# Turning the experts' rows and silu products on VectorE in 32x32 blocks, and moving a group's sums behind the next up products

## The chip, the cores and the metric

One of the eight cores of a Trainium2 chip runs the whole program, one launch of one decoder step of two layers. The time is device time in microseconds (us), from runs of the whole program. Engines: TensorE (PE) multiplies, VectorE (DVE) and ScalarE (ACT) do the elementwise work, GpSimd (POOL) gathers rows, SyncE (SP) issues the transfers of the weights. Each engine works through its own instructions in order, and they meet at semaphores.

## What is computed

Each layer is a mixer (gated DeltaNet in layer 0, differential attention in layer 1) followed by a mixture of experts. The change is in the experts, which run once in each layer, over 288 tokens (256 prompt rows and 8x4 sample rows), with all numbers in fp32:

```python
def hier_moe(xn, w_rg, b_rg, w_re, b_re, w_gate, w_up, w_down):
    ...                       # top-1 group of 4, then top-2 of its 8 experts; gate = softmax weights
    return routed_experts(xt, eidx, gate, w_gate, w_up, w_down)

def expert_block(args):       # inside routed_experts, for each block of rows of one expert
    xblk, e = args
    hid = jax.nn.silu(xblk @ w_gate[e]) * (xblk @ w_up[e])   # 1024 -> 512
    return hid @ w_down[e]                                   # 512 -> 1024
```

There are 32 experts, each with three matrices of 2 MB (1024x512, 1024x512, 512x1024). All 96 matrices of a layer are read once from HBM.

## The kernel before

`moe_phase` takes the experts two at a time: 16 **groups** a layer, numbered 0 to 15 (`LAST` is 15). A group has 128 row places, 64 for each of its two experts. A group runs as follows.

- **Gather.** GpSimd reads the group's rows from the normed activations in DRAM (`xn_dram`) into `xg`, 128 rows by 1024. It may start when the group before has been read out of `xg` (semaphore `gx_T`), and semaphore `gathered` tells of its landing.
- **Rows turned.** A product needs the row index on the free axis, so `rows_T` (L2516) has TensorE transpose `xg` in eight 128x128 pieces into PSUM (`ps_x`). VectorE and ScalarE each carry half of it to `xgT`, scaled by the norm gain on the way (`rows_kept`: DVE L2375, four pieces at once; ACT L2203, a piece at a time). They signal `gx0_kept` and `gx1_kept`.
- **Gate and up.** `stage` (L2539) multiplies `xgT` by the two experts' matrices into `ps_gate`, then into `ps_up`, each with half the array's columns. ScalarE takes the silu of `ps_gate` into `hid` (L2209), VectorE multiplies it by `ps_up` (`hidden`, L2381).
- **Silu products turned.** `hid_T` (L2548) transposes `hid` on TensorE in four pieces into `ps_hid`, and VectorE copies them to `hidT` (`turned`, L2386, signal `hid_kept`).
- **Down.** `products` (L2566) multiplies `hidT` by the down matrices into `ps_y`. VectorE and ScalarE each copy half to `y_sb` (L2404, L2219).
- **Sums.** VectorE builds the group's 0/1 selection matrix with the routing weights in it (`selection`, L2392 to L2399), TensorE transposes it (`sel_T`, L2575), and `combine` (L2582, L2585) multiplies it by `y_sb` into five PSUM areas, which VectorE adds to the residual (`add`, L2412 four times 128x512, L2416 four times 32x256).

The order is written out by hand, one list for each engine. In the steady part TensorE does for group g: `sel_T(g-1)`, gate(g), three of the sums of g-1, up(g), the fourth sum, `hid_T(g)`, the fifth sum, `rows_T(g+1)`, down(g). The sums of one group thus stand among the products of the next.

The weights come through a ring of ten 2 MB slots, `slots`. SP issues a load into a slot as soon as the product that read it last is done (`half_used`, `used`), so that up to ten matrices wait ahead of TensorE. `LAST` has an order of its own. Groups beyond the 16 exist only if an expert has more than 64 tokens; the trace has none.

## Time and profile before

| | us |
|---|---|
| median of 3 runs | 1524.02 (1522.5 to 1524.5) |
| the profiled run, its whole time | 1519.33 |
| its span, first to last instruction | 1517.4 |

How to read it: the page gives each engine's busy share over the whole span, and the 40 slices show that both TensorE and the DMA engines are at nine tenths in the two stretches of the experts (about 367 to 815 us and 1056 to 1505 us). A busy share doesn't say which of two full resources sets the end, so the rows below come from single stretches: windows over some groups, one group in order of time, and the first and last groups of both layers. A row of the timeline that merges instructions gives the time from the start of the first to the end of the last. An fp32 matmul is recorded as two pieces, so that 16 instructions of a stage show as x32.

### The profile page before, as it was taken

The numbers are of one execution on the slowest core, as the hardware profiler recorded it, in microseconds if no ns is written. First come the engines' busy times: TensorE is split into PE (matmuls) and PEld (weight loads), VectorE is DVE, ScalarE is ACT, GpSimd is POOL, SyncE is SP. The second block draws the span as 40 slices with busy tenths as digits, with TensorE's granted clock in tenths as the row PEclk, the third lists the DMA queues.
The fourth block names the chain that finished last, engine by engine and source line by source line (L and its number), as shares of the span: only waits on it lengthen the run. The fifth ranks groups of instructions, "written<-read, shape, count | busy, mean of one in ns | idle before, by whom it ended". The sixth has DMA issues, their size and how long they took to land. (4 is left out here: it accounts for less than half of the span.)

```text
span 1517.4 us, 20326 instructions
## 1 busy us (share of the span) xinstructions
PE 1470.7 (97%) x7727; PEld 738.4 (49%) x7727; DVE 634.6 (42%) x1657; ACT 285.0 (19%) x746; POOL 73.0 (5%) x123
## 2 busy tenths in 40 slices
PE   9999999999999999999999998899999999999995
PEld 8787878667333333333334445657333333333331
DVE  3666566445323323224244235735232322433324
ACT  2424244214110101001001004523010100110101
POOL 0101010001000000000000000001000000000000
PEclk9999999999999999999999999999999999999998
DMA  7432324467999999999999036785999999999993
GB/s 232 137 116 75 116 78 143 187 230 308 417 430 431 428 429 433 430 428 426 426 427 368 19 126 257 268 343 204 412 429 431 430 429 431 431 430 426 427 426 157
DMA packets 101504, 484.54 MB, mean 319 GB/s; under 512 B 16410, under 2 KB 51134, under 8 KB 67634
## 3 DMA queue, kind: packets, MB, share of 16 engines
q1 hardware_dynamic: 96818, 478.90, 78.0%
q0 software_dynamic: 4320, 4.42, 0.8%
q8 instruction: 54, 0.88, 0.2%
q14 instruction: 24, 0.20, 0.0%
q10 hardware_dynamic: 288, 0.14, 0.0%
HBM read 483.77 MB, written 10.97 MB: 326 GB/s over the span
## 5 line engine op out<-in xcount | busy, mean ns | idle before, releaser
L2539 PE MATMUL moe_ps_gate<-slots,moe_xrT 128*64 128x512 f32 x1024 | 228.1, 596 | 8.5 <-DMA slots<-in_w_gate_e_dram 8.5
L2539 PE MATMUL moe_ps_up<-slots,moe_xrT 128*64 128x512 f32 x1024 | 226.8, 595 | 0.0
L2566 PE MATMUL moe_ps_y<-slots,router_inputs 128*64 128x512 f32 x960 | 212.6, 595 | 0.0
L2412 DVE TENSOR_TENSOR resid<-resid,moe_ps_x 128x512 f32<-128x512 f32 x60 | 41.3, 688 | 252.7 <-PE moe_ps_x L2582 252.7
L2539 PEld LDWEIGHTS moe_ps_up<-slots,moe_xrT 128*64 128x64 f32 x1024 | 71.2, 137 | 150.9 <-issue 138.7
L2539 PEld LDWEIGHTS moe_ps_gate<-slots,moe_xrT 128*64 128x64 f32 x1024 | 72.2, 137 | 137.9 <-issue 136.7
L966 PE MATMUL gdn_bank<-gdn_xT,slots 128*128 128x288 f32 x512 | 136.3, 410 | 0.7 <-ACT slots L485 0.7
L2566 PEld LDWEIGHTS moe_ps_y<-slots,router_inputs 128*64 128x64 f32 x960 | 66.3, 137 | 124.9 <-issue 124.6
L2203 ACT ACTIVATE moe_xrT<-moe_ps_x,router_inputs 128x128 f32<-128x128 f32 x128 | 36.5, 367 | 379.1 <-PE moe_ps_x L2520 363.5
L966 PEld LDWEIGHTS gdn_bank<-gdn_xT,slots 128*128 128x128 f32 x512 | 92.6, 190 | 22.8 <-issue 1.1
L2381 DVE TENSOR_TENSOR router_inputs<-router_inputs,moe_ps_up 128x512 f32<-128x512 f32 x32 | 22.0, 688 | 195.0 <-PE moe_ps_up L2539 195.0
L2209 ACT ACTIVATE router_inputs<-moe_ps_gate 128x512 f32<-128x512 f32 x32 | 19.1, 597 | 220.9 <-PE moe_ps_gate L2539 220.9
L2582 PE MATMUL moe_ps_x<-moe_y_sb,router_inputs 128*128 128x512 f32 x120 | 59.5, 618 | 0.0
L2219 ACT COPY moe_y_sb<-moe_ps_y 128x512 f32<-128x512 f32 x32 | 18.7, 585 | 193.6 <-PE moe_ps_y L2566 176.6
L2404 DVE COPY moe_y_sb<-moe_ps_y 128x512 f32<-128x512 f32 x30 | 20.7, 692 | 81.3 <-PE moe_ps_y L2566 81.3
L2167 POOL DMA_INDIRECT moe_xrT<-xn_rows,moe_rows_in x30 | 30.9, 1029 | 471.9 <-PE moe_ps_x L2520 470.0
L2396 DVE TENSOR_SCALAR moe_place<-consts,moe_lpos,moe_gcur 128x128 f32<-128x128 f32 x192 | 52.1, 345 | 1.2
L2416 DVE TENSOR_TENSOR resid<-resid,moe_ps_up 32x256 f32<-32x256 f32 x112 | 46.2, 413 | 2.6
L1730 PE MATMUL at_bank<-slots,at_XK 128*128 128x512 f32 x96 | 42.0, 596 | 0.0
L1730 PE MATMUL at_pair<-slots,at_XK 128*128 128x512 f32 x96 | 41.8, 593 | 0.0
L709 DVE SCALAR_TENSOR_TENSOR slots<-slots,gdn_cw 128x312 f32<-128x312 f32 x72 | 39.2, 545 | 2.5
L2582 PEld LDWEIGHTS moe_ps_x<-moe_y_sb,router_inputs 128*128 128x128 f32 x120 | 20.3, 189 | 38.7 <-issue 38.7
(509 smaller groups left out, 1817.9 us busy)
## 6 DMA issues: line engine op xcount, KB each, us to landing
slots<-in_w_gate_e_dram SPq DMA_DIRECT2D x40, 2048.0 KB, 23.0
slots<-in_w_up_e_dram SPq DMA_DIRECT2D x40, 2048.0 KB, 22.8
slots<-in_w_down_e_dram SPq DMA_DIRECT2D x40, 2048.0 KB, 25.8
slots<-in_w_gate_e_dram SPq DMA_DIRECT2D x48, 1024.0 KB, 26.2
slots<-in_w_up_e_dram SPq DMA_DIRECT2D x48, 1024.0 KB, 26.6
slots<-in_w_down_e_dram SPq DMA_DIRECT2D x48, 1024.0 KB, 26.0
slots<-in_w_in_a_dram SPq DMA_DIRECT2D x16, 1024.0 KB, 5.8
slots<-in_w_kv_dram SPq DMA_DIRECT2D x4, 2048.0 KB, 20.6
```

The source lines that it names most:

```text
L709: ins = V.scalar_tensor_tensor(acc[:, a, j, 0:ACC_COLS], src, cw[:, a, j, tap:tap + 1], acc[:, a, j, 0:ACC_COLS], ALU.mult, ALU.add)
L966: last = T.matmul(PB[i % 2][:, 0:T_ALL], w4[:, j, k, 128 * a:128 * a + 128], xT[:, k, :], start=(k == 0), stop=(k == KT - 1))
L1730: last = T.matmul(bank[:, :], XK[:, 0 if j < 2 else 1, k, at[t]], wslot[3 * half + j][:, k, :], start=(k == 0), stop=(k == KT - 1))
L2167: pool.indirect_dma_start(xg, None, xn_dram[:, :], bass.IndirectOffsetOnAxis(rows_in[:, :], 0), bounds_check=T_ALL - 1, oob_is_err=False). ...
L2203: last = A.activation(xgT[:, k, :], ps_x[:, 1, k - 4, :], ACT.Copy, scale=norm_T[:, k:k + 1])
L2381: V.tensor_tensor(hid, hid, ps_up[:], ALU.mult).then_inc(s["hidden"], 1)
L2396: last = V.tensor_scalar(place[:, k, t, :], m["lanes"][:, :], where[:, k, t:t + 1], gcur[:, k, t:t + 1], ALU.is_equal, ALU.mult)
L2412: V.tensor_tensor(half, half, banks[i][:, :], ALU.add).then_inc(s["summed"], 1)
L2416: V.tensor_tensor(part, part, banks[i][32 * q:32 * q + 32, 0:256], ALU.add).then_inc(s["summed"], 1)
L2539: last = T.matmul(ps[64 * e:64 * e + 64, :], xgT[:, k, 64 * e:64 * e + 64], slots[:, slot[2 * n + e], 512 * k:512 * k + 512], start=(k == ...
L2566: last = T.matmul(ps_y[64 * e:64 * e + 64, h, :], hidT[:, k, 64 * e:64 * e + 64], slots[:, slot[4 + e], 1024 * k + 512 * h:1024 * k + 512 ...
L2582: last = T.matmul(banks[i][:, :], selT[:, at[t]], y_sb[:, 512 * h:512 * h + 512], start=True, stop=True)
```

## The change

- Except in group 0, the rows and the silu products are transposed by VectorE, from SBUF to SBUF, with no PSUM in between. `blocks_turned` issues 16 instructions, each of which takes 32 partitions by 4 pieces by 32 columns and turns its four 32x32 blocks; the block's place in the 128x128 piece is turned by the choice of source and destination partitions. Rows take two calls (32 instructions), the silu products one (16).
- The rows' gain is then applied in place by ScalarE (`rows_scaled`), eight instructions in place of four, in two halves.
- VectorE's order becomes: `hidden(g)`, `hid_turned(g)`, `rows_turned(g+1)`, all five `add(g-1)`, `selection(g)`, `kept(g)`.
- TensorE's order becomes: gate(g), `sel_T(g-1)`, up(g), all five sums of g-1, down(g). The fourth sum goes to the bank `ps_hid`, which the transposes no longer use. `LAST` mostly takes the same path as the others.
- `gx_T` is signalled by VectorE after the rows are turned. The loads of the weights and the semaphores that they wait for stay as they were.

```diff
+            def rows_scaled(g):
+                for n in range(2):
+                    act.wait_ge(*((s["gx_half"], g), (s["gx_T"], g + 1))[n])
+                    for k in range(4 * n, 4 * n + 4):
+                        last = A.activation(xgT[:, k, :], xgT[:, k, :], ACT.Copy, scale=norm_T[:, k:k + 1])
+                    last.then_inc((s["gx0_kept"], s["gx1_kept"])[n], 1)
...
             with act.Fori(1, LAST) as g:
+                silu(g)
                 sel_kept(g - 1, flat_hid)
-                silu(g)
-                rows_kept(g + 1)
+                rows_scaled(g + 1)
                 kept(g)
...
+            def blocks_turned(dst, src, ks):
+                for q in range(4):
+                    for a in range(4):
+                        last = V.transpose(dst[32 * q:32 * q + 32, ks, 32 * a:32 * a + 32], src[32 * a:32 * a + 32, ks, 32 * q:32 * q + 32])
+                return last
+
+            def rows_turned(g):
+                dve.wait_ge(s["gathered"], g * 16)
+                blocks_turned(xgT, xgv, slice(0, 4)).then_inc(s["gx_half"], 1)
+                blocks_turned(xgT, xgv, slice(4, KT)).then_inc(s["gx_T"], 1)
+
+            def hid_turned(g):
+                dve.wait_ge(s["hidden"], g + 1)
+                blocks_turned(hidT, hidv, slice(0, FT)).then_inc(s["hid_kept"], 1)
...
             with dve.Fori(1, LAST) as g:
-                for i in range(3):
-                    add(g - 1, i, ps_sum)
                 hidden(g)
-                turned(g)
-                for i in range(3, 5):
+                hid_turned(g)
+                rows_turned(g + 1)
+                for i in range(5):
                     add(g - 1, i, ps_sum)
-                rows_kept(g + 1)
                 selection(g, False, lpos, gcol[:, :, :, bass.ds(g, 1)].rearrange("p k t o -> p k (t o)"))
                 kept(g, s["y_made"])
...
             def gate_up(g, slot, filled):
-                pe.wait_ge(s["hid_kept"], g)
-                sel_T(g - 1, flat_hid)
                 pe.wait_ge(s["silued"], g)
-                if not (isinstance(g, int) and g == 1):
-                    pe.wait_ge(s["summed"], g * 8 - 12)
                 stage(g, 0, ps_gate, slot, filled)
-                outputs_kept(g - 1)
-                for i in range(3):
-                    combine(g - 1, i, ps_sum)
                 pe.wait_ge(s["hidden"], g)
                 if not (isinstance(g, int) and g == 1):
                     pe.wait_ge(s["summed"], g * 8 - 8)
+                sel_T(g - 1, flat_hid)
                 stage(g, 1, ps_up, slot, filled)
-                pe.wait_ge(s["silued"], g + 1)
-                combine(g - 1, 3, ps_sum)
-                hid_T(g)
+                outputs_kept(g - 1)
+                for i in range(4):
+                    combine(g - 1, i, ps_sum)
+                pe.wait_ge(s["hidden"], g + 1)
                 combine(g - 1, 4, ps_sum)
-                pe.wait_ge(s["summed"], g * 8 - 6)
...
                     gate_up(g, slot, later)
-                    rows_T(g + 1)
                     products(g, slot, later)
```

TensorE's order in group 1, which all later groups but the last repeat. Before (`moe_ps_hid<-consts,moe_place` is `sel_T`, `moe_ps_hid<-consts,router_inputs` is `hid_T`, `moe_ps_x<-consts,moe_xrT` is `rows_T`, what reads `moe_y_sb` are the sums):

```order
L2575 MATMUL moe_ps_hid<-consts,moe_place 128x128 x2
L2575 MATMUL moe_ps_hid<-consts,moe_place 128x32
L2539 MATMUL moe_ps_gate<-slots,moe_xrT 64x512 x16
L2582 MATMUL moe_ps_x<-moe_y_sb,router_inputs 128x512 x2
L2582 MATMUL moe_ps_tab<-moe_y_sb,router_inputs 128x512
L2539 MATMUL moe_ps_up<-slots,moe_xrT 64x512 x16
L2582 MATMUL moe_ps_gate<-moe_y_sb,router_inputs 128x512
L2548 MATMUL moe_ps_hid<-consts,router_inputs 128x128 x4
L2585 MATMUL moe_ps_up<-moe_y_sb,router_inputs 32x256 x4
L2520 MATMUL moe_ps_x<-consts,moe_xrT 128x128 x8
L2566 MATMUL moe_ps_y<-slots,router_inputs 64x512 x16
```

And now, at the same place of the program:

```order
L2555 MATMUL moe_ps_gate<-slots,moe_xrT 64x512 x16
L2591 MATMUL moe_ps_hid<-consts,moe_place 128x128 x2
L2591 MATMUL moe_ps_hid<-consts,moe_place 128x32
L2555 MATMUL moe_ps_up<-slots,moe_xrT 64x512 x16
L2598 MATMUL moe_ps_x<-moe_y_sb,router_inputs 128x512 x2
L2598 MATMUL moe_ps_tab<-moe_y_sb,router_inputs 128x512
L2598 MATMUL moe_ps_hid<-moe_y_sb,router_inputs 128x512
L2601 MATMUL moe_ps_up<-moe_y_sb,router_inputs 32x256 x4
L2582 MATMUL moe_ps_y<-slots,router_inputs 64x512 x16
```

Both kinds of transposes of data are gone, the selection's transpose stands between gate and up, and all sums stand between up and down.

VectorE's order from `hidden` on, in its loop over groups 1 to 14. Before (the adds L2412 of the first three sums stand ahead of this piece, `kept` L2404 behind it; `router_inputs` holds `hid` and `hidT`):

```order
L2381 TENSOR_TENSOR router_inputs<-router_inputs,moe_ps_up 128x512
L2386 COPY router_inputs<-moe_ps_hid 128x512
L2408 REGISTER_ALU
L2412 TENSOR_TENSOR resid<-resid,moe_ps_gate 128x512
L2408 REGISTER_ALU
L2416 TENSOR_TENSOR resid<-resid,moe_ps_up 32x256 x4
L2374 REGISTER_ALU
L2375 TENSOR_TENSOR moe_xrT<-moe_ps_x,router_inputs 128x512
L2392 ISA
L2392 COPY moe_gcur<-moe_gcol 128x6
L2396 TENSOR_SCALAR moe_place<-consts,moe_lpos,moe_gcur 128x128 x6
L2399 TENSOR_TENSOR moe_place<-moe_place 128x384
```

And now (the fourth and fifth adds, the four instructions 32x256, and the selection follow behind this piece):

```order
L2408 TENSOR_TENSOR router_inputs<-router_inputs,moe_ps_up 128x512
L2390 STREAM_TRANSPOSE router_inputs<-router_inputs 32x4x32 x16
L2395 REGISTER_ALU
L2390 STREAM_TRANSPOSE moe_xrT<-moe_xrT 32x4x32 x32
L2435 ISA
L2439 TENSOR_TENSOR resid<-resid,moe_ps_x 128x512
L2435 REGISTER_ALU
L2439 TENSOR_TENSOR resid<-resid,moe_ps_x 128x512
L2435 REGISTER_ALU
L2439 TENSOR_TENSOR resid<-resid,moe_ps_tab 128x512
```

Two instructions of 128x512 (L2386, L2375) have become 48 of 32x4x32, and they stand ahead of the adds and of the selection.

## Rows read from the trace of the kernel before

**Rows 1.** The page: engine, busy us (share of the span), instructions.
```profile
PE 1470.7 (97%) x7727; PEld 738.4 (49%) x7727; DVE 634.6 (42%) x1657; ACT 285.0 (19%) x746; POOL 73.0 (5%) x123
```

**Rows 2.** Windows of layer 0; behind POOL: granted clock, DMA share, GB/s.
```profile
563.50:591.00 27.50, 27.50 (x128) 9.89 (x128) 9.26 (x20) 2.67 (x7) 1.20 (x2) 1.00 1.01 430
701.00:729.00 28.00, 27.58 (x127) 9.91 (x127) 9.25 (x20) 2.67 (x7) 1.20 (x2) 1.00 1.02 427
729.00:759.00 30.00, 27.94 (x130) 10.43 (x128) 9.26 (x20) 2.67 (x7) 1.02 (x1) 1.00 1.01 425
759.00:788.00 29.00, 27.38 (x127) 10.26 (x127) 9.26 (x20) 2.67 (x7) 0.00 (x0) 1.00 1.01 427
```

**Rows 3.** Timeline of one middle group: start, length in us, engine, what [idle before].
```profile
566.19 7.09 PE L2539 MATMUL moe_ps_up<-slots,moe_xrT 128*64 128x512 f32 x32
...
573.20 1.12 PE L2582 MATMUL moe_ps_gate<-moe_y_sb,router_inputs 128*128 128x512 f32 x2
573.32 0.69 DVE L2381 TENSOR_TENSOR router_inputs<-router_inputs,moe_ps_up 128x512 f32<-128x512 f32 x1 [6.34 <-PE moe_ps_up L2539]
...
574.85 0.69 DVE L2386 COPY router_inputs<-moe_ps_hid 128x512 f32<-128x512 f32 x1 [0.84 <-PE moe_ps_hid L2548]
...
575.46 0.68 DVE L2412 TENSOR_TENSOR resid<-resid,moe_ps_gate 128x512 f32<-128x512 f32 x1
576.05 1.74 DVE L2416 TENSOR_TENSOR resid<-resid,moe_ps_up 32x256 f32<-32x256 f32 x4
...
576.33 7.09 PE L2566 MATMUL moe_ps_y<-slots,router_inputs 128*64 128x512 f32 x32
576.44 1.14 ACT L2203 ACTIVATE moe_xrT<-moe_ps_x,router_inputs 128x128 f32<-128x128 f32 x4 [12.31 <-PE moe_ps_x L2520]
...
577.25 1.02 POOL L2167 DMA_INDIRECT moe_xrT<-xn_rows,moe_rows_in  x1 [17.12 <-PE moe_ps_x L2520]
...
578.43 0.16 DVE L2392 COPY moe_gcur<-moe_gcol 128x6 f32 x1
...
578.63 1.63 DVE L2396 TENSOR_SCALAR moe_place<-consts,moe_lpos,moe_gcur 128x128 f32<-128x128 f32 x6
...
580.29 0.56 DVE L2399 TENSOR_TENSOR moe_place<-moe_place 128x384 f32<-128x384 f32 x1
...
583.35 0.61 PE L2575 MATMUL moe_ps_hid<-consts,moe_place 128*128 128x128 f32 x3
...
583.89 7.09 PE L2539 MATMUL moe_ps_gate<-slots,moe_xrT 128*64 128x512 f32 x32
...
587.40 0.18 POOL L2163 COPY moe_rows_in<-moe_table 128x1 uint32 x1 [9.13 <-DMA moe_xrT<-xn_rows,moe_rows_in]
```

**Rows 4.** Timeline: down products of groups 0 and 15, both layers; gate 15's second half.
```profile
383.85 7.09 PE L2566 MATMUL moe_ps_y<-slots,router_inputs 128*64 128x512 f32 x32
...
801.95 7.09 PE L2554 MATMUL moe_ps_y<-slots,router_inputs 128*64 128x512 f32 x32 [0.78 <-DVE router_inputs L2386]
...
1072.98 7.09 PE L2566 MATMUL moe_ps_y<-slots,router_inputs 128*64 128x512 f32 x32
...
1474.20 3.65 PE L2539 MATMUL moe_ps_gate<-slots,moe_xrT 128*64 128x512 f32 x16 [1.22 <-DMA slots<-in_w_gate_e_dram]
...
1491.39 7.09 PE L2554 MATMUL moe_ps_y<-slots,router_inputs 128*64 128x512 f32 x32 [0.78 <-DVE router_inputs L2386]
```

**Rows 5.** VectorE lines: duration ns min/median/max, first and last start; and a timeline row.
```profile
L2416 DVE TENSOR_TENSOR resid<-resid,moe_ps_up x112: 399/415/424, 411.1 to 1462.3; 32x256 f32<-32x256 f32 x112
L2316 DVE TENSOR_SCALAR moe_place<-consts,moe_lpos x12: 279/282/288, 361.1 to 1051.2; 128x128 f32<-128x128 f32 x12
361.12 1.27 DVE L2316 TENSOR_SCALAR moe_place<-consts,moe_lpos 128x128 f32<-128x128 f32 x6
```

**Rows 6.** Behind the experts of layer 0: TensorE's timeline, and a window.
```profile
815.73 2.61 PE L1717 MATMUL at_pair<-consts,resid 128*128 128x128 f32 x13 [2.29 <-PEq L2722]
815.00:820.00 5.00, 4.28 (x25) 3.94 (x25) 2.83 (x5) 4.06 (x7) 0.00 (x0) 0.66 1.01 363
```

More of the change, by code:

```diff
@@ L2048, in by_tile @@
             return x.rearrange("p (k c) -> p k c", k=KT)
+        xgv = by_tile(xg)
+        hidv = hid.rearrange("p (c k) -> p k c", k=FT)
         used = [s["gate_made"], s["up_made"], s["y_made"]]
@@ L2381, in hidden, with first_turned @@
                 V.tensor_tensor(hid, hid, ps_up[:], ALU.mult).then_inc(s["hidden"], 1)
-            def turned(g):
-                dve.wait_ge(s["hid_T"], g + 1)
+            def first_turned():
+                dve.wait_ge(s["hid_T"], 1)
                 V.tensor_copy(hidT, ps_hid[:]).then_inc(s["hid_kept"], 1)
@@ L2425, in _ @@
             V.tensor_scalar(table_o[:].rearrange("p a c -> p (a c)"), ps_over, NOWHERE, None, ALU.add).then_inc(s["over_ready"], 1)
-            turned(0)
-            rows_kept(1)
+            first_turned()
+            rows_turned(1)
             selection(0, True, lpos, gcol[:, :, :, 0])
@@ L2430, in _ @@
             with dve.Fori(1, LAST) as g:
-                for i in range(3):
+                hidden(g)
+                hid_turned(g)
+                rows_turned(g + 1)
+                for i in range(5):
                     add(g - 1, i, ps_sum)
-                hidden(g)
-                turned(g)
-                for i in range(3, 5):
-                    add(g - 1, i, ps_sum)
-                rows_kept(g + 1)
                 selection(g, False, lpos, gcol[:, :, :, bass.ds(g, 1)].rearrange("p k t o -> p k (t o)"))
                 kept(g, s["y_made"])
-            for i in range(5):
-                add(LAST - 1, i, ps_sum_14)
             selection(LAST, False, lpos, gcol[:, :, :, LAST])
             hidden(LAST)
-            turned(LAST)
+            hid_turned(LAST)
+            for i in range(5):
+                add(LAST - 1, i, ps_sum)
             dve.wait_ge(s["y_h0"], 1)
@@ L2462, in _ @@
                     g = o + MAIN_GROUPS
-                    rows_kept(g)
+                    rows_turned(g)
                     hidden(g)
-                    turned(g)
+                    hid_turned(g)
                     selection(g, False, olow, gcol_o[:, :, :, bass.ds(o, 1)].rearrange("p k t o -> p k (t o)"))
@@ L2512, in _ @@
                 T.matmul(ps_count, ones[0:rows[t], :], both[0:rows[t], t, :], start=(t == 0), stop=(t == NT - 1))
-            xgv = by_tile(xg)
-            hidv = hid.rearrange("p (c k) -> p k c", k=FT)
-            def rows_T(g):
-                pe.wait_ge(s["gathered"], g * 16)
-                for k in range(KT):
-                    last = T.transpose(ps_x[:, k // 4, k % 4, :], xgv[:, k, :], ident[:, :])
-                last.then_inc(s["gx_T"], 1)
             def landed(half, i, slot, filled):
@@ L2542, in stage, with first_hid_T @@
                         last.then_inc((half_used, used)[k // 4][n], 1)
-            def hid_T(g):
-                pe.wait_ge(s["hidden"], g + 1)
+            def first_hid_T():
+                pe.wait_ge(s["hidden"], 1)
                 for k in range(FT):
@@ L2643, in _ @@
             last.then_inc(s["extras_made"], 1)
-            hid_T(0)
-            rows_T(1)
+            first_hid_T()
             products(0, slot, filled)
@@ L2649, in _ @@
             gate_up(1, slot, filled)
-            rows_T(2)
             products(1, slot, filled)
@@ L2662, in _ @@
                 gate_up(g, slot, filled)
-                rows_T(g + 1)
                 products(g, slot, filled)
             slot, filled = pieces(LAST)
-            pe.wait_ge(s["hid_kept"], LAST)
-            sel_T(LAST - 1, flat_hid)
-            pe.wait_ge(s["silued"], LAST)
-            pe.wait_ge(s["summed"], 8 * LAST - 12)
-            stage(LAST, 0, ps_gate, slot, filled)
-            outputs_kept(LAST - 1)
-            for i in range(5):
-                if i == 3:
-                    pe.wait_ge(s["silued"], LAST + 1)
-                combine(LAST - 1, i, ps_sum_14)
-            pe.wait_ge(s["hidden"], LAST)
-            pe.wait_ge(s["summed"], 8 * LAST - 8)
-            stage(LAST, 1, ps_up, slot, filled)
-            pe.wait_ge(s["summed"], 8 * LAST)
-            sel_T(LAST, flat_x[0])
-            hid_T(LAST)
+            gate_up(LAST, slot, filled)
+            pe.wait_ge(s["silued"], MAIN_GROUPS)
+            sel_T(LAST, ps_gate)
             pe.wait_ge(s["hid_kept"], MAIN_GROUPS)
@@ L2710, in _ @@
                     pe.wait_ge(s["summed"], g * 8)
-                    rows_T(g)
                     stage(g, 0, ps_gate, slot, filled)
                     stage(g, 1, ps_up, slot, filled)
-                    hid_T(g)
                     products(g, slot, filled)
```

26 lines of the change are left out of this document (13 added, 13 removed).

## The prediction

> **What bounds the kernel now.** The page comes first, for the shares: TensorE is busy 97% of the span, VectorE 42% [rows 1]. Alone that says "take work off TensorE and give it to VectorE". The second view, windows over single groups, shows two limits side by side. In a middle group TensorE has no idle time in 27.5 us, and the DMA engines are full as well, at 430 GB/s [rows 2]. A group reads six matrices of 2 MB, 12.6 MB, which takes 29.3 us at that rate. TensorE is thus 1.8 us a group faster than the weights, and lives on the matrices that stand ready in the ring. After twelve groups that lead is spent: the windows from 701 us on show TensorE idle in part and 28 to 30 us a group, with the DMA as full as before. TensorE's wait of 1.22 us for a gate matrix in group 15 says the same [rows 4]. Third, the two layers' ends: from down(0) to down(15) it is 801.95 - 383.85 = 418.1 us in layer 0 and 1491.39 - 1072.98 = 418.4 us in layer 1 [rows 4], that is 27.9 us a step. That sum is set by the weights, since the DMA was full all the way.
>
> Two things follow. TensorE time that is taken away in the middle only spends the lead sooner. And a chain that needs more than about 27.9 us a group becomes the new bound, whichever engine it runs through.
>
> **What leaves TensorE.** `hid_T` and `rows_T` leave; together with the sums around them they stood between up and down, 573.20 to 576.33 = 3.1 us [rows 3]. All five sums now stand there instead. A 128x512 sum is two pieces of about 0.43 us (32 such pieces fill a stage's 7.0 us with two side by side, 16 x 0.43), so four take 3.4 us and the fifth about 0.6 us: 4.0 us. The three sums between gate and up go, `sel_T` with 0.54 us (583.35 to 583.89) comes. TensorE alone would need 3 x 7.01 + 0.54 + 4.0 = 25.6 us a group, 1.9 us under 27.5. By itself that is worth nothing, as the weights need 29.3.
>
> **What comes to VectorE.** 16 transposes of the silu products and 32 of rows a group; L2386 and L2375, some 0.6 us each, go. Call x the time from one transpose's start to the next. No transpose on VectorE is in the trace, so x is bounded by rows. Instructions of 128 elements a partition last 0.282 us, and six in a row take 1.27 us, so each starts (1.27 - 0.28)/5 = 0.198 us after the one before: they overlap by 0.085 us [rows 5]. The low end is x = 0.20. The four adds of 32x256 do not overlap: (1.74 - 0.415)/3 = 0.442 us from start to start at 0.415 us each [rows 3, 5]. They move from one 32-partition block to the next, as each of the 48 transposes does (its source block changes every time). With twice a transpose's elements they are the high end, x = 0.44. I take the nearest: 128 elements, 0.28 us, plus the gap of 0.03 us that the adds show instead of an overlap, 0.31 us. A turned block can't put out its first column before its 32nd input column has come, which at the adds' pace of about 1 ns an element is another 0.03 us. So x = 0.34.
>
> The trace's contrast between L2316 and L2416 is what the Trainium skill describes (VectorE: DVE Perf Modes, section Two Vector instructions with no wait between them): an instruction whose input or output starts in another quadrant of 32 partitions than the last one's is held until all earlier ones are done. Without the hold the sum below would stay at the weights' limit. The same page speaks against this change (section The three transpose paths): VectorE yields a grid of separately turned 32x32 blocks, and a full 128x128 belongs on TensorE. It gives 311 ns for 128x128 in bf16 on VectorE; as an estimate from that page, with the gap of the adds, x would be 0.34 too, if fp32 costs the same, which no run here shows.
>
> **The new chain, one group.** VectorE now does everything in one row, and TensorE's up products wait for its end, because `sel_T(g-1)` needs the selection, and the selection stands behind the rows and the adds. From the end of up(g-1): `hidden` starts 0.12 us later and takes 0.69 [rows 3]; 0.04 to the first transpose; 16x for the silu products, whereupon down(g-1) starts; 32x for the rows; four adds at 0.6 (575.46 to 576.05) and the 32x256 ones 1.8, together 4.2; the selection from 578.43 to 580.29 + 0.56, 2.4. Then about 0.1 to TensorE, `sel_T` 0.54, and up(g) 7.01. Sum: 15.1 + 48x. At x = 0.34 this is 31.4 us, more than the weights' 29.3 and than the 27.9 of before.
>
> TensorE's branch beside it is shorter. Down and gate together end 14.0 us after down starts; the selection is there after 32x + 6.6 = 17.5 us. The rows' first half is ready for gate at 16x + 1.2 = 6.6 us, under down's 7.0 (ScalarE's four pieces took 1.14 us [rows 3]). The second half comes at 32x + 1.2 = 12.1 us, where gate wants it at 10.5. That stall of 1.6 us ends gate at 15.6, still ahead of the selection, so it is hidden; were the selection early, the chain would run here.
>
> TensorE will idle about 1.6 us in gate, 1.9 us before `sel_T`, and 6.3 - 4.0 = 2.3 us before down. ScalarE's four extra activations end before `kept` is wanted. The gather now starts 32x = 10.9 us into down instead of 0.9 (577.25 against 576.33) and took about 10 us (577.25 to 587.40) [rows 3]; its rows are wanted 31 us into it, so 10 us are left and it costs nothing. SP's loads wait on the same products as before; with a slower TensorE they start later, but they then have 2 us a group to spare.
>
> **The sum.** The step from down(0) to down(1) has no adds in it: rows' second half 32x + 1.2, half a gate 3.5, `sel_T` 0.6, up 7.0, `hidden` 0.85, 16x: 13.15 + 48x = 29.5 us. Fourteen more steps of 31.4 give 469.1 us, where 418.1 and 418.4 stood. Each layer gets 51 us longer. Behind down(15) little changes: its matrices have long landed, the adds of group 14 (4.2 us) fit beside its 7.0 us, and the last sums are the same. In general both layers together change by 2 x (224.6 + 720x - 418.25) = 1440x - 387 us, zero at x = 0.27. At 0.34 it is +102 us. The profiled run took 1519.3 us with 1517.4 of span; it would take 1621. The median of the runs shown is 4.7 us above it, so I predict **1626 us**. With x from 0.30 to 0.37 it is 1569 to 1670.
>
> **Rivals.**
> - *The weights keep setting the end* (x at or below 0.27: no hold, or a fast transpose). For it speak the full DMA queues in every window. Against it: the adds of 32x256 do not overlap. In the tail, gate 15's second half lands at 1474.2 [rows 4], up's last matrices two 2 MB later, 4.2 MB at 427 GB/s = 9.8 us, thus 1484.0; then 3.5 of up, 0.85, and 16 x 0.2 give down(15) at 1491.6, where 1491.39 stood. The time would be 1522 to 1527: not slower, and hardly faster either. The point that decides is 15.1 + 48x = 27.9.
> - *A moderate transpose*, x about 0.28, held but quick: 1440 x 0.28 - 387 = +16, 1540 us.
> - *TensorE's clock falls in the new gaps.* After an idle time of 2.29 us a stretch of 5 us ran at a mean granted clock of 0.66, part of it at the lower level of 1.2 GHz, and lost 5 x 0.34 = 1.7 us [rows 6]. Gaps of 1.22 us in the experts left it at full. The new gaps are between. In down the loss would be hidden, in up it would not; once for each of 28 groups it adds 48 us: 1674.
> - *A dear transpose*, x from 0.38 to 0.44 (fp32 at a lower pace than an add): 1684 to 1770.
>
> **How the numbers follow.** Forecast 0.58; clock on top of it (1630 to 1720) 0.12; dear 0.07; moderate 0.08; weights set the end, within 0.2%, 0.12; faster by over 0.2% (a gain in the tail that I can't see) 0.03. About 0.2%, 3 us, is what a measurement of this kernel can tell from no change. The range from 1535 to 1710 holds the forecast, the moderate case, nearly all of the clock's and some of the dear one, 0.8 in all. Slower: 0.58 + 0.12 + 0.07 + 0.08 = 0.85.
>
> **What would show it.** Each step: the start-to-start time of 16 transposes gives x (5.4 us for 16); silu to silu in the middle 31.4 us in place of 27.50; TensorE idle before `sel_T`, released by VectorE's last selection instruction; TensorE idle before down, released by the transposes; no wait for a gate matrix in groups 13 to 15; DMA share below 1. The forecast is wrong if silu to silu is below 28 us (then x was small, and groups 13 to 15 still wait for DMA), or if the up products last more than 7.1 us (then it is the clock).

## The result, and the profile after

The changed kernel takes 1636.60 us (median of 4 runs, 1636.04 to 1637.49), beside 1523.26 us for the kernel before on the same chip: 1.0746 times as long, 95% interval 1.0727 to 1.0764. The forecast was 1626 us, within a range of 1535 to 1710. The direction was right and the size was 11 us short. The profiled execution took 1636.44 us with a span of 1634.6, and the numbers below are from it.

First the page: busy time and share of the span, by engine. They answer to [rows 1].

```profile
PE 1464.8 (90%) x7367; PEld 712.7 (44%) x7367; DVE 1068.7 (65%) x3037; ACT 325.6 (20%) x866; POOL 73.0 (4%) x123
```

TensorE is busy hardly less (part of that at its lower clock, see below), VectorE 434 us more, and no engine is as full as TensorE was. That points to a chain that runs through several engines. The windows of 32 us, about a step each, in the same columns as [rows 2], say that it isn't the weights either:

```profile
581.00:613.00 32.00, 28.82 (x125) 9.77 (x123) 23.90 (x68) 3.97 (x11) 1.21 (x2) 0.95 0.94 388
613.00:645.00 32.00, 27.74 (x119) 9.12 (x117) 23.98 (x68) 4.02 (x11) 1.21 (x2) 0.95 1.00 416
677.00:709.00 32.00, 28.82 (x131) 9.59 (x129) 23.84 (x68) 3.96 (x11) 1.21 (x2) 1.00 0.91 377
```

The DMA engines have pauses (share 0.91 to 1.00, 377 to 416 GB/s), TensorE too, and the granted clock falls in some windows. The chain itself is seen in the timeline of one step (start, length, engine, line, operation, idle before it and releaser). Lines of the changed kernel: L2408 is `hidden`, L2390 the transposes, L2582 down, L2555 gate and up, L2212 the gain put on by ScalarE, L2439 and L2443 the adds, L2423 and L2426 the selection, L2591 `sel_T`, L2598 and L2601 the sums, L2168 the gather.

```profile
598.58 1.98 PE L2598 MATMUL moe_ps_x<-moe_y_sb,router_inputs 128*128 128x512 f32 x4
598.70 0.69 DVE L2408 TENSOR_TENSOR router_inputs<-router_inputs,moe_ps_up 128x512 f32<-128x512 f32 x1 [7.15 <-PE moe_ps_up L2555]
599.42 6.55 DVE L2390 STREAM_TRANSPOSE router_inputs<-router_inputs 32x128 f32<-32x128 f32 x16
...
602.21 0.64 PE L2601 MATMUL moe_ps_up<-moe_y_sb,router_inputs 128*32 128x256 f32 x8
606.00 10.12 DVE L2390 STREAM_TRANSPOSE moe_xrT<-moe_xrT 32x128 f32<-32x128 f32 x32
...
606.03 8.78 PE L2582 MATMUL moe_ps_y<-slots,router_inputs 128*64 128x512 f32 x32 [3.18 <-DVE router_inputs L2390]
...
611.09 1.28 ACT L2212 ACTIVATE moe_xrT<-moe_xrT,router_inputs 128x128 f32<-128x128 f32 x4 [19.02 <-DVE moe_xrT L2390]
...
614.64 7.04 PE L2555 MATMUL moe_ps_gate<-slots,moe_xrT 128*64 128x512 f32 x32
...
616.16 1.28 DVE L2439 TENSOR_TENSOR resid<-resid,moe_ps_x 128x512 f32<-128x512 f32 x2
...
616.97 1.02 POOL L2168 DMA_INDIRECT moe_xrT<-xn_rows,moe_rows_in  x1 [20.75 <-DVE moe_xrT L2390]
...
618.56 1.75 DVE L2443 TENSOR_TENSOR resid<-resid,moe_ps_up 32x256 f32<-32x256 f32 x4
...
622.08 0.56 DVE L2426 TENSOR_TENSOR moe_place<-moe_place 128x384 f32<-128x384 f32 x1
...
622.79 0.58 PE L2591 MATMUL moe_ps_hid<-consts,moe_place 128*128 128x128 f32 x3 [1.11 <-DVE moe_place L2426]
...
623.30 4.94 PE L2555 MATMUL moe_ps_up<-slots,moe_xrT 128*64 128x512 f32 x22
...
627.89 0.18 POOL L2164 COPY moe_rows_in<-moe_table 128x1 uint32 x1 [9.89 <-DMA moe_xrT<-xn_rows,moe_rows_in]
```

From 598.70 to 622.64 VectorE works without a pause: product, 16 transposes, 32 transposes, adds, selection. TensorE waits for it twice, before down and before `sel_T`. (The up products at 623.30 are cut off by the window, hence x22.) The table of TensorE's waits over the whole run (us in total, times, longest) shows the first wait in all 28 down products of groups 1 to 14 and the second before 24 of the 28 `sel_T` behind them. In the other four a down product of 9.8 to 10.1 us had used it up:

```profile
PE moe_ps_y L2582 <- DVE router_inputs L2390: 89.4, 28, 3.4
PE moe_ps_hid L2591 <- DVE moe_place L2426: 30.8, 24, 1.6
PE moe_ps_gate L2555 <- ACT moe_xrT L2212: 6.5, 7, 1.0
```

No product waits for a matrix any more, whereas [rows 4] had such a wait. The two layers' ends, answering to [rows 4], are the down products of groups 0 and 15:

```profile
384.98 8.78 PE L2582 MATMUL moe_ps_y<-slots,router_inputs 128*64 128x512 f32 x32 [0.78 <-DVE router_inputs L2413]
...
860.05 8.66 PE L2570 MATMUL moe_ps_y<-slots,router_inputs 128*64 128x512 f32 x32 [2.65 <-DVE router_inputs L2390]
...
1134.16 7.09 PE L2582 MATMUL moe_ps_y<-slots,router_inputs 128*64 128x512 f32 x32 [0.78 <-DVE router_inputs L2413]
...
1608.58 7.09 PE L2570 MATMUL moe_ps_y<-slots,router_inputs 128*64 128x512 f32 x32 [2.63 <-DVE router_inputs L2390]
```

Layer 0 takes 475.1 us and layer 1 474.4, against 418.1 and 418.4: 57.0 + 56.0 = 113.0 of the span's 117.2 us. The rest lies outside the steps: 1.1 us ahead of the first down products, and 3.1 us between the layers (860.05 to 1134.16 is 274.1 us, against 271.0). The four rows name part of it: each down(0) waits 0.78 us for VectorE's copy, where `rows_T` used to fill that time, and down(15) of layer 0 takes 8.66 us in place of 7.09.

Last the transposes by themselves (ns min/median/max, first and last start):

```profile
L2390 DVE STREAM_TRANSPOSE moe_xrT<-moe_xrT x960: 289/303/309, 384.8 to 1586.6; 32x128 f32<-32x128 f32 x192
L2390 DVE STREAM_TRANSPOSE router_inputs<-router_inputs x480: 391/395/420, 409.0 to 1608.1; 32x128 f32<-32x128 f32 x160
```

There are two prices. From start to start it is 10.12/32 = 0.317 us for the rows and about 6.55/16 = 0.41 us for the silu products.

### The profile page after: what moved, and what is told of

It reads as the page before. It is cut to its first block and busy times, and to the rows that moved or that the text cites. A ratio compares the mean times of both kernels' runs of the same rounds, so it can differ in the third digit from the quotient of the medians.

```text
span 1634.6 us, 21002 instructions
## 1 busy us (share of the span) xinstructions
PE 1464.8 (90%) x7367; PEld 712.7 (44%) x7367; DVE 1068.7 (65%) x3037; ACT 325.6 (20%) x866; POOL 73.0 (4%) x123
## 5 line engine op out<-in xcount | busy, mean ns | idle before, releaser
L2582 PE MATMUL moe_ps_y<-slots,router_inputs 128*64 128x512 f32 x960 | 254.9, 692 | 91.0 <-DVE router_inputs L2390 89.4
L2390 DVE STREAM_TRANSPOSE moe_xrT<-moe_xrT 32x128 f32<-32x128 f32 x960 | 290.7, 303 | 14.1
L2555 PE MATMUL moe_ps_gate<-slots,moe_xrT 128*64 128x512 f32 x1024 | 226.9, 593 | 6.5 <-ACT moe_xrT L2212 6.5
L2555 PE MATMUL moe_ps_up<-slots,moe_xrT 128*64 128x512 f32 x1024 | 226.7, 595 | 0.0
L2212 ACT ACTIVATE moe_xrT<-moe_xrT,router_inputs 128x128 f32<-128x128 f32 x240 | 76.7, 390 | 674.6 <-DVE moe_xrT L2390 674.6
L2390 DVE STREAM_TRANSPOSE router_inputs<-router_inputs 32x128 f32<-32x128 f32 x480 | 190.3, 396 | 7.0
L2582 PEld LDWEIGHTS moe_ps_y<-slots,router_inputs 128*64 128x64 f32 x960 | 77.7, 158 | 255.7 <-issue 166.2
L2408 DVE TENSOR_TENSOR router_inputs<-router_inputs,moe_ps_up 128x512 f32<-128x512 f32 x32 | 22.0, 688 | 224.8 <-PE moe_ps_up L2555 224.8
L2555 PEld LDWEIGHTS moe_ps_gate<-slots,moe_xrT 128*64 128x64 f32 x1024 | 73.6, 137 | 153.0 <-issue 133.9
L2555 PEld LDWEIGHTS moe_ps_up<-slots,moe_xrT 128*64 128x64 f32 x1024 | 70.9, 137 | 130.3 <-issue 129.1
L2598 PE MATMUL moe_ps_x<-moe_y_sb,router_inputs 128*128 128x512 f32 x120 | 59.5, 618 | 0.0
L2168 POOL DMA_INDIRECT moe_xrT<-xn_rows,moe_rows_in x30 | 30.9, 1031 | 588.2 <-DVE moe_xrT L2390 586.3
L2423 DVE TENSOR_SCALAR moe_place<-consts,moe_lpos,moe_gcur 128x128 f32<-128x128 f32 x192 | 52.1, 342 | 1.2
L2443 DVE TENSOR_TENSOR resid<-resid,moe_ps_up 32x256 f32<-32x256 f32 x120 | 49.6, 413 | 2.8
L2591 PE MATMUL moe_ps_hid<-consts,moe_place 128*128 128x128 f32 (+1 forms) x90 | 17.7, 274 | 30.8 <-DVE moe_place L2426 30.8
L2439 DVE TENSOR_TENSOR resid<-resid,moe_ps_x 128x512 f32<-128x512 f32 x60 | 38.5, 683 | 0.9
```

Source lines behind the costliest of these rows:

```text
L2168: pool.indirect_dma_start(xg, None, xn_dram[:, :], bass.IndirectOffsetOnAxis(rows_in[:, :], 0), bounds_check=T_ALL - 1, oob_is_err=False). ...
L2212: last = A.activation(xgT[:, k, :], xgT[:, k, :], ACT.Copy, scale=norm_T[:, k:k + 1])
L2390: last = V.transpose(dst[32 * q:32 * q + 32, ks, 32 * a:32 * a + 32], src[32 * a:32 * a + 32, ks, 32 * q:32 * q + 32])
L2423: last = V.tensor_scalar(place[:, k, t, :], m["lanes"][:, :], where[:, k, t:t + 1], gcur[:, k, t:t + 1], ALU.is_equal, ALU.mult)
L2439: V.tensor_tensor(half, half, banks[i][:, :], ALU.add).then_inc(s["summed"], 1)
L2443: V.tensor_tensor(part, part, banks[i][32 * q:32 * q + 32, 0:256], ALU.add).then_inc(s["summed"], 1)
```

## Experiments

**Theory**: the step is the length of VectorE's row, and 48 held transposes make it longer than the weights' time. **Rivals**: the new order of the sums costs the time; TensorE's clock, which falls in the new gaps, costs it; a transpose is dear for another reason than the hold. Every ratio is to the kernel before on the same chip. "Step" is from one down start to the next.

### The order alone

The kernel before, with its transposes on TensorE, but `sel_T` behind gate and the three sums behind up. ScalarE takes the silu and VectorE the product first, as in the changed kernel. The part for TensorE:

```diff
-                sel_T(g - 1, flat_hid)
                 pe.wait_ge(s["silued"], g)
...
                 stage(g, 0, ps_gate, slot, filled)
-                outputs_kept(g - 1)
-                for i in range(3):
-                    combine(g - 1, i, ps_sum)
...
+                sel_T(g - 1, flat_hid)
                 stage(g, 1, ps_up, slot, filled)
+                outputs_kept(g - 1)
+                for i in range(3):
+                    combine(g - 1, i, ps_sum)
```

> The kernel before with the other part of the change alone: in groups 1 to 14 all five sums and sel_T stand as in the changed kernel (sel_T between gate and up, sums behind up), while TensorE still turns rows and silu products, and the fourth sum keeps the gate bank. Theory (the weights set the end, and the order of the sums is worth nothing by itself): TensorE needs about 26.7 to 27.5 us a group, less than the weights' 27.9, so 1520 to 1526 us. Rival (the sums behind up are part of the loss): the sums and transposes between up and down grow to 5.7 us, and if adds and banks then stall TensorE the step passes 27.9 and the time 1530.

Measured 1523.35 us, 1.0009 [0.9998, 1.0019]. Steps of 27.14 us, until the weights run out. TensorE's waits then:

```profile
PE moe_ps_up L2539 <- DMA slots<-in_w_up_e_dram: 15.2, 14, 2.4
```

With the transposes on TensorE, this order neither costs nor gives anything. A step 0.4 us shorter than 27.5 only turns into waits for matrices.

### Rows on VectorE, silu products back on TensorE

`hid_turned` is replaced by four TensorE transposes between the second and the third sum, and one VectorE copy:

```diff
-                hid_turned(g)
+                later_turned(g)
...
-                for i in range(4):
+                for i in range(2):
+                    combine(g - 1, i, ps_sum)
+                later_hid_T(g)
+                for i in range(2, 5):
                     combine(g - 1, i, ps_sum)
```

> The changed kernel with the silu products of groups 1 to 15 back on TensorE (four transposes into the gate bank, between the second and the third sum, and one copy by VectorE); rows stay on VectorE. Theory (the chain through VectorE sets the step): from the end of up, hidden and its transposes and copy take 3.2 us, the rows 10.1, adds and selection 6.7, sel_T and up 7.6: 27.6 us a step, which is below the 27.9 that the weights allow, so the weights set the end again: 1519 to 1532 us. Rival (the 32 row transposes, two thirds of the new work, are what is dear whatever stands around them, or VectorE's SBUF traffic slows others): two thirds of the loss stay, about 1595 us.

Measured 1525.01 us, 1.0012 [0.9997, 1.0027]; steps of 27.4 us, then waits for matrices again:

```profile
PE moe_ps_up L2560 <- DMA slots<-in_w_up_e_dram: 12.3, 10, 2.3
```

Two thirds of VectorE's transposes stand in this kernel at the same 0.303 us each, and they cost nothing. Without the missing third VectorE does 6.55 - 0.69 = 5.9 us less, but it now stands still for TensorE's transposes ahead of its copy:

```profile
601.99 0.69 DVE L2413 COPY router_inputs<-moe_ps_gate 128x512 f32<-128x512 f32 x1 [1.68 <-PE moe_ps_gate L2570]
```

From `hidden` to the rows it is 3.0 us (599.62 to 602.60 in this trace) in place of 7.3 (598.70 to 606.00), so the row is 4.3 us shorter, as the step is. 3.8 of them reach the weights' 27.9 us, and the rest turns into waits for matrices.

### The selection ahead of the silu product

```diff
             with dve.Fori(1, LAST) as g:
+                selection(g, False, lpos, gcol[...])
                 hidden(g)
                 hid_turned(g)
                 rows_turned(g + 1)
                 for i in range(5):
                     add(g - 1, i, ps_sum)
-                selection(g, False, lpos, gcol[...])
                 kept(g, s["y_made"])
```

> The changed kernel with one step moved on VectorE: the selection of group g stands ahead of hidden(g) instead of behind the adds, so it is built while the up products run and VectorE idles. Theory (TensorE's up products wait for the end of VectorE's row of work, of which the selection is the last 2.4 us): the step from down to down falls from 31.73 us to between 30.0 (full clock; then the rows' second half, 10.1 + 1.35 + half a gate 3.5 behind down's start, ends gate at 15.0) and 30.7 (if down keeps running at the low clock), so 1588 to 1608 us. Rival (VectorE's total work, 24.7 us of 31.7, or the transposes in themselves set the step, in whatever order they stand): the step stays at 31.7, 1636 us. Second rival (weights): no change either.

Measured 1600.91 us, 1.0512 [1.0492, 1.0532]. Steps 30.57 us. Waits before `sel_T` are gone, and one before down remains; timeline of a step:

```profile
629.01 8.78 PE L2582 MATMUL moe_ps_y<-slots,router_inputs 128*64 128x512 f32 x32 [3.17 <-DVE router_inputs L2390]
...
637.63 7.04 PE L2555 MATMUL moe_ps_gate<-slots,moe_xrT 128*64 128x512 f32 x32
...
644.60 0.61 PE L2591 MATMUL moe_ps_hid<-consts,moe_place 128*128 128x128 f32 x3
```

2.4 us of selection left VectorE's row, yet the step lost only 1.2: TensorE's branch (gap, down, gate, up) is next at 30.6. In it down runs partly at the lower clock (8.78 instead of 7.09 us), which counts here. In three steps where it ran at full clock, gate waited 0.95 us for its second half instead, and the step was 30.05. One step, with a down of 10.03 us, took 31.83.

### The silu products stored tile by tile

The silu products lie in memory with the four pieces interleaved, so that a transpose reads every fourth number, 16 bytes apart. Here they are stored piece by piece; silu and product read PSUM with that stride instead.

```diff
-        hidv = hid.rearrange("p (c k) -> p k c", k=FT)
+        hidv = hid.rearrange("p (k c) -> p k c", k=FT)
...
-                A.activation(hid, ps_gate[:], ACT.Silu).then_inc(s["silued"], 1)
+                A.activation(hidv, ps_gate[:].rearrange("p (c k) -> p k c", k=FT), ACT.Silu).then_inc(s["silued"], 1)
...
-                V.tensor_tensor(hid, hid, ps_up[:], ALU.mult).then_inc(s["hidden"], 1)
+                V.tensor_tensor(hidv, hidv, ps_up[:].rearrange("p (c k) -> p k c", k=FT), ALU.mult).then_inc(s["hidden"], 1)
```

> The changed kernel with the silu products laid out piece by piece in SBUF (ScalarE and VectorE read PSUM with a stride of 4 elements, and the transposes read 32 elements that lie side by side). Theory: the 16 transposes of the silu products cost 0.41 us each against 0.317 for those of the rows because their source has a stride of 16 bytes; laid side by side they cost 0.32, the step falls by 16 x 0.09 = 1.5 us to 30.2, and the time by 30 x 1.5 = 45 us to 1592. If the strided PSUM reads are dearer (0.6 us more in hidden), 1.5 becomes 0.9 and the time 1610. Rival (they are dearer because they read what was just written, or for their place behind hidden): they stay at 0.41, 1636 us.

Measured 1598.36 us, 1.0493 [1.0476, 1.0511]. Its transposes of silu products, and two rows of its timeline:

```profile
L2390 DVE STREAM_TRANSPOSE router_inputs<-router_inputs x480: 299/303/308, 408.6 to 1568.6; 32x128 f32<-32x128 f32 x160
```

```profile
612.43 8.78 PE L2555 MATMUL moe_ps_up<-slots,moe_xrT 128*64 128x512 f32 x32
...
621.98 5.05 DVE L2390 STREAM_TRANSPOSE router_inputs<-router_inputs 32x128 f32<-32x128 f32 x16
```

Now both kinds cost the same, 5.05 us for 16: the stride was worth 1.5 us a group. The product and the silu, which read PSUM with that stride now, did not get longer (0.69 and 0.60 us). Steps are 30.24 us, as the sum says (31.73 - 1.5), except in 6 groups where **up** ran partly at the lower clock: 31.93.

The Trainium skill (SBUF — State Buffer, Specifications) says that SBUF has lines of 16 bytes and that full bandwidth needs two hits a line or more. A stride of 16 bytes has one. The two measurements agree with that, at a price of 92 ns for 128 fp32 elements; that the lines are the reason is not shown by itself.

### Both edits, and rows in one call

The selection ahead and the silu products in tiles, together:

> The changed kernel with both edits: selection ahead of hidden, and the silu products laid out in tiles. Theory (chain): from the end of up 5.95 us to down, the rows' second half and half a gate end 15.0 us behind down's start, sel_T and up take 7.6: 28.5 us a step at full clock, 29.1 if down runs at the low clock. Layers 14 x 28.5 + 28.4 = 427 to 436 us against 475 now, so 1540 to 1560 us; the gains of the two edits (35.7 and 38.2 us) would give 1563 if they simply added up with their clock falls. Rival (VectorE's total of 23 us a group or the weights' queue, which is not full at this pace): above 1575.

Measured 1542.32 us, 1.0131 [1.0109, 1.0154], steps of 28.56 us. Two falls of the clock in down are left.

Then the silu products in tiles and the selection at its old place, with the rows' two calls made one, so that 16 instructions turn eight pieces each:

```diff
-                blocks_turned(xgT, xgv, slice(0, 4)).then_inc(s["gx_half"], 1)
-                blocks_turned(xgT, xgv, slice(4, KT)).then_inc(s["gx_T"], 1)
+                blocks_turned(xgT, xgv, slice(0, KT)).then_inc(s["gx_T"], 1)
...
-                    act.wait_ge(*((s["gx_half"], g), (s["gx_T"], g + 1))[n])
+                    act.wait_ge(s["gx_T"], g + 1)
```

> The kernel with silu products stored tile by tile, and on top the rows turned by 16 instructions of 256 elements a partition (all eight pieces of a block at once) in place of 32 of 128; ScalarE scales both halves only when all are turned. Question: is a transpose's 0.303 us a fixed cost for the held instruction, or does it grow with its elements? If most of it is fixed and an element adds about 1 ns: 0.303 + 0.13 = 0.44 us, 16 in about 7.2 us instead of 10.1. VectorE's row then needs 30.24 - 2.9 = 27.3 us, and TensorE's becomes the longer one: from down's start 7.2 for the rows, 1.2 for ScalarE's first half, 7.0 gate, 0.5, 7.0 up, 0.84, 5.05 for the silu products: 28.8 us a step, in all about 1550 us. If the cost is by the block turned (twice the pieces cost twice the time, 0.62 us from start to start): 16 in 9.9 us, the first half is scaled 11.1 us behind down's start, steps of 31.6 us, 1635 us.

Measured 1556.18 us, 1.0227 [1.021, 1.0244]; steps of 28.9 to 29.2 us. The rows' transposes, and the wait that is the next limit:

```profile
L2390 DVE STREAM_TRANSPOSE moe_xrT<-moe_xrT x480: 422/436/442, 384.2 to 1504.8; 32x256 f32<-32x256 f32 x160
```

```profile
617.28 7.18 DVE L2390 STREAM_TRANSPOSE moe_xrT<-moe_xrT 32x256 f32<-32x256 f32 x16
...
625.83 2.37 PE L2554 MATMUL moe_ps_gate<-slots,moe_xrT 128*64 128x512 f32 x10 [1.44 <-ACT moe_xrT L2212]
```

128 more elements cost 0.133 us, about 1.04 ns each. On a straight line through the two sizes, 0.303 us is 0.17 us of fixed cost and 0.133 us of work. 32 rows' instructions took 10.12 us, 16 of twice the size 7.18. The theory of a fixed part holds. In return the whole of gate waits, 1.44 us, and TensorE's branch sets the step.

### Every block turned in its own place

The source block takes the destination's partitions, so that both ends of an instruction stay in one 32-partition block for four instructions in a row. The blocks are turned but not moved, so this kernel computes other products; its instructions are the same in number and size.

```diff
-V.transpose(dst[32 * q:32 * q + 32, ks, 32 * a:32 * a + 32], src[32 * a:32 * a + 32, ks, 32 * q:32 * q + 32])
+V.transpose(dst[32 * q:32 * q + 32, ks, 32 * a:32 * a + 32], src[32 * q:32 * q + 32, ks, 32 * a:32 * a + 32])
```

> The changed kernel with each 32x32 block turned within its own 32 partitions instead of moved to others: same count, sizes and strides, but the source and destination partitions change only at every fourth instruction (the blocks so end in the wrong place; that part of the computation is changed). Theory (an instruction that starts in other partitions than the last waits for its end, others overlap by 0.085 us): three of four start 0.115 us sooner, 16 take 5.2 instead of 6.55 us and 32 take 7.3 to 7.8 instead of 10.1; the step falls to about 28.4 us and the time by about 96 us to 1541. Rival (a transpose holds its array until it is empty, so none overlaps): spacing stays at 0.317 and 0.41, 1636 us.

Measured 1526.46 us, 1.0026 [1.001, 1.0042]. Its rows' transposes by themselves, and in the timeline:

```profile
L2390 DVE STREAM_TRANSPOSE moe_xrT<-moe_xrT x960: 256/261/309, 384.6 to 1475.2; 32x128 f32<-32x128 f32 x192
```

```profile
577.05 7.19 DVE L2390 STREAM_TRANSPOSE moe_xrT<-moe_xrT 32x128 f32<-32x128 f32 x32
```

32 take 7.19 us in place of 10.12: 0.22 us each, against 0.317. The 16 of the silu products take 5.11 in place of 6.55. That is more than expected, since three of four instructions are also recorded as shorter (medians of 256 to 266 ns by place among the 16, for 303); the first of each four, which changes its block, still takes 300 to 307. Steps are 27.45 us until the weights run out. The edit takes away two things, the change of block from one instruction to the next and the move of a block to other partitions. The trace of the changed kernel tells them apart: four of its sixteen transposes leave their block in its own partitions, and at 299 to 307 ns they are no shorter than their neighbours. So the change of block is what makes the rows' transposes miss their overlap, and with most of it gone the kernel ends 0.3% above the one before. This is the rule that the prediction took from the Trainium skill (VectorE: DVE Perf Modes, Two Vector instructions with no wait between them), now seen on transposes.

### TensorE's clock

TensorE runs part of down at the lower of its two levels (1.2 and 2.4 GHz) in 24 of the changed kernel's 32 down products: mostly 8.78 us in place of 7.09. The window over the first 4 us of the down product shown above has a mean granted clock of 0.66:

```profile
606.00:610.00 4.00, 3.97 (x12) 1.20 (x14) 3.83 (x13) 0.00 (x0) 0.00 (x0) 0.66 1.02 438
```

Three kernels fill its gaps with multiplications of constants, nothing else changed (12 ahead of down; 7 ahead of `sel_T`; both), and a fourth has both with 10 instead of 12.

```diff
+                pe.wait_ge(s["silued"], g + 1)
+                keep_busy(12)
```

```diff
+                keep_busy(7, ps_up)
                 sel_T(g - 1, flat_hid)
```

> The changed kernel with 12 matmuls of 128x128 on constants added behind the fifth sum (into the gate bank, which is free there; nothing reads them), about 2.8 us of TensorE work in the 3.16 us in which it idles ahead of down. Theory (the falls of TensorE's clock follow that gap, and their loss of 1.7 us lies in down and gate, beside VectorE's longer branch, so that it costs nothing): down lasts 7.1 us in all groups, the step stays at 31.73, the time at 1634 to 1638 us. Rival (the clock is part of the loss): the time falls by up to 20 falls x 1.7 = 34 us, to about 1603.

12 ahead of down: 1661.18 us, 1.0912 [1.0895, 1.0928], slower than the change itself; both theories missed. Down runs at full clock, and the fall has moved:

```profile
613.42 7.09 PE L2582 MATMUL moe_ps_y<-slots,router_inputs 128*64 128x512 f32 x32 [0.35 <-DVE router_inputs L2390]
...
630.70 8.78 PE L2555 MATMUL moe_ps_up<-slots,moe_xrT 128*64 128x512 f32 x32
```

17 of the 30 up stages behind group 0 are long, and those steps take 33.5 us. Up is on the chain, down is not: a fall costs 1.7 us in up and next to nothing in down (0.15 us in two steps of the changed kernel, whose downs took 10.1 us).

> The changed kernel with only the second filling, 7 matmuls between gate and sel_T. Theory: the gap of 3.16 us ahead of down remains, so the clock may still fall in down or gate, where VectorE's branch is longer and hides it; up stays at 7.09 us; step 31.73, time 1634 to 1640 us. Rival (any filling moves the falls into up): 1655 or more.

7 ahead of `sel_T`: 1652.27 us, 1.0848 [1.0823, 1.0872], neither the theory's time nor the rival's reason. Up stays at full clock, down doesn't, and after a late down the filling itself is in the way:

```profile
592.72 0.56 DVE L2426 TENSOR_TENSOR moe_place<-moe_place 128x384 f32<-128x384 f32 x1
...
593.61 1.83 PE L2527 MATMUL moe_ps_up<-consts 128*128 128x128 f32 x14
...
595.28 0.56 PE L2591 MATMUL moe_ps_hid<-consts,moe_place 128*128 128x128 f32 x3
```

The selection was ready at 593.28, and `sel_T` comes 2.0 us later, behind the filling. The expectation had left this out.

> The changed kernel with TensorE's two longest gaps filled by matmuls on constants that nothing reads: 12 ahead of down, as before, and 7 (1.7 us) between gate and sel_T, into the up bank, which is free there. With the first gap alone filled the low clock had moved from down, where it costs nothing, into 17 of the 30 later up products, 8.78 us each instead of 7.09, and the time had risen to 1661 us. Theory (the falls come from the sum of the gaps in a stretch, and cost only where TensorE's products lie on the chain, in up): with the gap ahead of up filled too, up stays at 7.09 us in all groups, the step is 31.7 to 32.0 and the time 1634 to 1642 us, as without any filling. Rival (the filling itself costs: its matmuls delay sel_T or the sums, or share power or ports with the others): it stays at 1655 or more.

Both: 1645.62 us, 1.0806 [1.0781, 1.0831]. Behind group 0 all stages but one run at full clock and nearly all steps take 31.7 us, as expected, but one of layer 1 took 41.2: TensorE stands still in a gate stage with nothing shown as released, and falls to the lower clock.

```profile
1333.19 0.77 PE L2555 MATMUL moe_ps_gate<-slots,moe_xrT 128*64 128x512 f32 x1 [2.48 <-issue]
1338.62 9.62 PE L2555 MATMUL moe_ps_gate<-slots,moe_xrT 128*64 128x512 f32 x31 [4.65 <-issue]
```

The DMA view of the stretch from 1326 to 1343 us has one thing that stands out: four packets of 16 KB of the queue for instructions (packets, MB, share), at 1327.2, 1330.4, 1336.3 and 1342.2 us, where the groups around have one in 21 to 28 us. Whether TensorE waited for them is not shown.

```profile
q8 instruction: 4, 0.07, 1.4%
```

> The kernel with both of TensorE's gaps filled, but with 10 multiplications ahead of down instead of 12. Question: in the version with 12, one step of layer 1 took 41.2 us instead of 31.7, with TensorE idle for 2.48 and 4.65 us and nothing shown as released; is it tied to filling the gaps, or to where that version's instructions happen to lie? If it is the place: no such step here, all steps 31.7 us, about 1636 us, the time of the change itself. If it comes with filled gaps: a step of some 41 us again, about 1645 us.

Both, with 10: **1634.40 us**, 1.0737 [1.0719, 1.0755]. No such step; all steps are 31.5 to 31.9 us. The mean granted clock of the changed kernel and, below it, of this one:

```profile
core 0: 1634.6 us, clock 0.965
```

```profile
core 0: 1632.8 us, clock 0.995
```

So with no falls left the kernel is 2 us faster, which the intervals don't separate from none, and not in the steps: from down(0) to down(15) it is 475.4 and 475.5 us here, 475.1 and 474.4 there. The gain lies between the layers (271.4 us here, 274.1 there); 1.6 of these 2.7 us are down(15) of layer 0, which no longer takes 8.66. The pause of the version before doesn't come with every filling of the gaps, and this version has no packet of the instruction queue in that stretch; what it is stays open.

## Why the prediction was right, and where it was off

- **What bounds before: right.** Four kernels with steps of 27.1 to 27.5 us (before, the order alone, rows only, blocks in place) all end within 0.3% of the kernel before, with waits for matrices late in a layer. The weights are the floor.
- **What leaves TensorE: nearly right.** Expected 25.6 us of its own work a step. Of the step that begins at 606.03, 31.71 us long, 3.18 and 1.11 are waits and 1.7 is lost to the clock, which leaves 25.7.
- **The price x: right on average, wrong in its parts.** Taken was 0.34 for all 48. Measured: 32 at 0.317 and 16 at 0.41, mean 0.348. The rows' 0.317 is a length of 0.303 and a gap of 0.014, where the working had 0.28, a gap of 0.03 and 0.03 for the 32nd column: held, as assumed, with half of the extras. What the working missed is the stride of 16 bytes under the silu products. That the two errors nearly cancel is luck: without the stride the kernel takes 1598.4 us, 28 below the forecast.
- **The chain: right.** 15.1 + 16 x 0.41 + 32 x 0.317 = 31.8 us; the steps are 31.73. Expected 31.4; silu to silu is the same.
- **The first step: half right.** 29.94 us in layer 1, against 29.5 expected. In layer 0 it was 30.56, since down(0) ran partly at the lower clock (8.78 us, the row above), and in that step, without adds, TensorE's branch sets the end.
- **TensorE's gaps: right in place, off in size.** Expected 1.6 in gate, 1.9 before `sel_T`, 2.3 before down. Measured 0.95, 1.64 and 3.2 us; the first only, and the second in full only, where down ran at full clock. The one before down is 0.9 us longer because 16x is 6.6 us, not 5.4, less 0.3 for sums that take 4.3 us, not 4.0; it is the gap after which the clock falls.
- **The clock as a rival: right in its condition.** "In down the loss would be hidden, in up it would not" is what the runs show. In the changed kernel the falls are in down, so that they cost next to nothing in the steps; the rival's 48 us would need them in every up. The kernel with silu products in tiles, with shorter gaps, does have some in up.
- **Gather, ScalarE, weights: right.** The gather is issued 10.9 us into down and landed 21.9 us into it, 10 us ahead of its use. No product waits for DMA.
- **The sum.** The term that was mis-sized is 48x: steps 0.35 us longer, twice 14 of them, 10 us; 1.5 for the two first steps. 4.2 us outside the steps were put at nothing: twice 0.8 before down(0), 1.6 in down(15) of layer 0 at the lower clock, and 1 us that no row here explains. Together 15 us on the profiled execution (1636.4 against 1621). The median is nearer, 1636.6 against 1626, because the profiled run before had been 4.7 us below its median and this one isn't, which is luck too.

The parts don't add up: 4.3 us out of VectorE's row (silu products back on TensorE) and 4.4 us (blocks in place) both end at the weights' limit, some 110 us lower. 3.9 us (selection ahead, products in tiles) shorten the step by 3.2 and end 94 us lower, at TensorE's branch. No version beats the kernel before. Rows alone on VectorE equal it (1525.0), and the best that turns both there, with the blocks moved to their places, takes 1542.3.

## What to carry to other kernels

Before moving work to the engine with the lower busy share, add up the row that it will then do between two products that wait for each other; 65% busy was enough to set the end here. If a layout change needs 32-partition blocks to move, count a fixed 0.17 us (fp32, as here) and no overlap for each instruction, make instructions long, and look at the stride of what they read. Where a resource outside the engines (here the weights' stream) sets the floor, a step shorter than it was worth nothing here, and a step longer than it cost its full excess in every group.

## What the runs showed of the hardware

- A VectorE transpose of a 32-partition block, fp32: 303 ns for 128 elements a partition and 436 ns for 256; 395 ns where the source in SBUF is read with a stride of 16 bytes. The same stride in PSUM cost a product of 128x512 nothing (0.69 us both ways). From start to start of a transpose 0.317 us if the block of partitions changes each time, 0.22 us on average if it changes every fourth time; three of four are then 256 to 266 ns long.
- Filling TensorE's longest gap did not keep its clock up here, it moved the fall to a later one: with 3.2 us filled, up fell behind a gap of 1.64 us in 17 of 30 groups, after which it had never fallen in the changed kernel. With gaps of 1.7 and 1.44 us and no third (rows in one call) no stage was longer than 7.09 us; with 1.7 and 0.95 us (both edits) two down products were.
- One program stood still for over 7 us inside a stage, with nothing that the profile shows to wait for, and didn't in a version with two multiplications fewer.
